# A two-block transformer on one core: the first pair's fourth weight sum by accumulating transfer, in all five feed-forward layers

## The reference, cut to what matters

```
gate, up = split(x @ w_gate_up)          # 1024 -> 2 * 2816
h = h + norm((silu(gate) * up) @ w_down) # 2816 -> 1024 (the first layer has no norm here)
```

## Time and profile before

| | |
|---|---|
| median of three executions | 1267.11 us |
| the profiled execution's own time | 1267.36 us |
| its span, first to last instruction | 1265.5 us |
| TensorE busy | 1250.5 us, 99% |
| VectorE busy | 1042.0 us, 82% |
| ScalarE busy | 804.2 us, 64% |
| granted TensorE clock, mean | 1.00 |
| moved by transfers | 277.32 MB, mean 219 GB/s |

### The profile page before, as it was taken

One profiled execution on the slowest core, in us unless ns is written; L12 is line 12 of the kernel. 1 busy time (PEld: TensorE's weight loads), 2 busy tenths in 40 slices (PEclk: granted clock), 3 DMA queues, 4 the chain that ended last, 5 costly groups with the idle time before them and its releaser, 6 DMA issues.

```text
span 1265.5 us, 15538 instructions
## 1 busy us (share of the span) xinstructions
PE 1250.5 (99%) x5897; PEld 1029.7 (81%) x5897; DVE 1042.0 (82%) x1035; ACT 804.2 (64%) x986; POOL 194.5 (15%) x224
## 2 busy tenths in 40 slices
PE   9999999999999999999999999999999999999998
PEld 7888878888888878888788888888888877788886
DVE  6766689999789996757799997999977568999984
ACT  6674576666576664645766664766656467766662
POOL 6142130110001100202201101111001003301100
PEclk9999999999999999999999999999999999999999
DMA  9537498997649955568979978389745535999931
GB/s 335 174 101 227 131 315 255 260 270 262 199 144 252 268 171 196 177 238 204 330 248 245 273 249 262 118 239 274 218 166 179 182 123 172 314 288 260 266 135 45
DMA packets 143002, 277.32 MB, mean 219 GB/s; under 512 B 8992, under 2 KB 39896, under 8 KB 142928
## 3 DMA queue, kind: packets, MB, share of 16 engines
q1 hardware_dynamic: 120192, 229.67, 51.5%
q0 software_dynamic: 22288, 45.54, 19.4%
q10 hardware_dynamic: 448, 1.12, 0.2%
HBM read 275.24 MB, written 1.05 MB: 218 GB/s over the span
## 4 chain that ended last, share of the span: by engine, by line
PE 83%; DVE 10%; issue 3%; ACT 3%; DMA 1%; POOL 0%; DVEq 0%; POOLq 0%; SPq 0%; ACTq 0%
PE B L2102 14%; PE B L2104 14%; PE B L2103 14%; PE B L2560 7%; PE B L2558 7%; PE B L2559 7%; DVE w_lo L1359 5%; PE T L2102 3%; PE T L2104 3%; PE T L2103 3%; PE T L2582 1%; DVE VD L1378 1%; ACT w_hi L768 1%; ACT w_hi L1082 1%; DMA VD<-in_ffn_w_gu 1%
## 5 line engine op out<-in xcount | busy, mean ns | idle before, releaser
L1359 DVE TENSOR_TENSOR w_lo<-w_raw,w_hi 128x2048 fp32r<-128x2048 f32 x129 | 296.5, 2300 | 87.2 <-ACT w_hi L768 86.9
L768 ACT ACTIVATE w_hi<-w_raw 128x2048 fp32r<-128x2048 f32 x129 | 247.2, 1919 | 103.2 <-PE B L2560 60.7
L2102 PE MATMUL B<-w_hi,xt_lo 128*128 128x512 f32 x652 | 260.2, 399 | 4.3 <-DVE w_lo L1359 2.2
L2104 PE MATMUL B<-w_hi,xt_hi 128*128 128x512 f32 x652 | 254.5, 390 | 0.0
L2103 PE MATMUL B<-w_lo,xt_hi 128*128 128x512 f32 x652 | 254.1, 390 | 0.0
L2558 PE MATMUL B<-w_hi,act_lo 128*128 128x512 f32 x440 | 172.5, 392 | 0.6 <-DVE w_lo L1359 0.6
L2560 PE MATMUL B<-w_hi,act_hi 128*128 128x512 f32 x440 | 171.4, 390 | 0.0
L2559 PE MATMUL B<-w_lo,act_hi 128*128 128x512 f32 x440 | 171.3, 389 | 0.0
L2102 PEld LDWEIGHTS B<-w_hi,xt_lo 128*128 128x128 f32 x652 | 122.5, 188 | 34.6 <-issue 4.4
L2104 PEld LDWEIGHTS B<-w_hi,xt_hi 128*128 128x128 f32 x652 | 122.4, 188 | 26.2
L2103 PEld LDWEIGHTS B<-w_lo,xt_hi 128*128 128x128 f32 x652 | 122.6, 188 | 23.2
(11 more groups left out here) (330 smaller groups left out, 2113.1 us busy)
## 6 DMA issues: line engine op xcount, KB each, us to landing
w_raw<-in_ffn_w_down SPq DMA_DIRECT2D x88, 512.0 KB, 5.7
Z<-in_ffn_w_gu SPq DMA_DIRECT2D x64, 512.0 KB, 7.8
w_raw<-in_ffn_w_gu SPq DMA_DIRECT2D x48, 512.0 KB, 5.1
nat<-in_ffn_w_gu SPq DMA_DIRECT2D x32, 512.0 KB, 7.7
QT<-in_ffn_w_gu SPq DMA_DIRECT2D x32, 512.0 KB, 7.0
Z<-in_ffn_w_gu POOLq DMA_DIRECT2D x32, 512.0 KB, 8.6
w_raw<-in_conv_w_in SPq DMA_DIRECT2D x24, 512.0 KB, 4.9
...
```

Of the source, the lines that this page charges most:

```text
L768: act.activation(whi[home(u)][:, :], raw[slot][:, :], ACT.Copy).then_inc(w_hi, 1)
L1359: dve.tensor_tensor(wlo[home(u)][:, :], src, whi[home(u)][:, :].bitcast(F32), ALU.subtract).then_inc(w_lo, 1)
L2102: pe.matmul(bank[:, :], lo[:, k, x], whi[s][:, c], start=first, stop=False, skip_group_check=more)
L2104: return pe.matmul(bank[:, :], hi[:, k, x], whi[s][:, c], start=False, stop=last, skip_group_check=more)
```

## The change

T4 of p = 0 joins those that are formed by an accumulating transfer, in all five layers (`FIRST_T4`). VectorE's sum for it is gone, GpSimd issues two more transfers of 512 KB in each layer, after the split of P6, and SyncE's load of the next B21 no longer waits for T4. Besides this, some orders are different: VectorE splits N1b ahead of `x_sums` (in all layers but the second), and the total of the activations is taken in two halves in layer 0 also; ScalarE does the first gate ahead of the high part of the activations' sums, loads the table of Silu earlier with a small instruction in layers 0 and 4, and in layer 4 squares h after N1b's split; ahead of layer 2 the split of N0b stands between the two halves of the squares and of the update; ahead of layer 4 the split of N0a stands ahead of `heads_lo(3)`, and TensorE's products of the output projection stand in another order.

The diff, cut to what the text speaks of:

```diff
--- before.py
+++ after.py
@@ -64,11 +64,17 @@
 
 SUMS = ((1, "T1"), (1, "T2"), (2, "T1"), (2, "T2"), (3, "T1"), (3, "T2"), (3, "T4"))
 ADDED_T4 = (1, 2)
+FIRST_T4 = (0, 1, 2, 3, 4)
+
+
+def added_t4(f):
+
+    return ((0,) if f in FIRST_T4 else ()) + ADDED_T4
 
 
 def sums_of(f):
 
-    return (((0, "T1"), (0, "T2")) if f % 2 else ()) + ((0, "T4"),) + SUMS
+    return (((0, "T1"), (0, "T2")) if f % 2 else ()) + (() if f in FIRST_T4 else ((0, "T4"),)) + SUMS
 
 
 def sums_ready(f, p, name):
@@ -78,7 +84,7 @@
 
 def t4_added(f, p):
 
-    return 32 * (len(ADDED_T4) * f + ADDED_T4.index(p) + 1)
+    return 32 * (sum(len(added_t4(g)) for g in range(f)) + added_t4(f).index(p) + 1)
 
 
 def down_block(name, p):
...
@@ -446,7 +453,7 @@
 
                     if p + 1 < SQUARES or next_gu is not None:
                         sp.wait_ge(w_lo, u0 + OP[reader, p] - 1)
-                        if name == "B21" and p == 0:
+                        if name == "B21" and p == 0 and f not in FIRST_T4:
                             sp.wait_ge(t_ok, sums_ready(f, 0, "T4"))
                         block_in(name, (p + 1) % SQUARES, w_gu if p + 1 < SQUARES else next_gu)
 
@@ -625,9 +632,11 @@
 
             def add_blocks(f, w_gu, p0=0):
 
+                if p0 and 0 in added_t4(f):
+                    add_block("T4", f, 0, w_gu)
                 for p in range(p0, SQUARES):
                     add_block("T3", f, p, w_gu)
-                    if p in ADDED_T4:
+                    if p in added_t4(f):
                         add_block("T4", f, p, w_gu)
 
             def post_gain(b, layer, i):
...
@@ -794,12 +803,14 @@
                 waits = [(in_x[t], 16)] * 2 if reader == "x" else [(h_up, h_ready(reader, t, half)) for half in range(2)]
                 tok_squares(stat, lambda t, half: h[:, t, half * HALF:half * HALF + HALF], t, waits)
 
-            def sum_squares(stat, reader, u_last, late_split=None, gain=0, pairs=PAIR, early=4):
-
-
-
-                tok_squares(stat, lambda t, half: pairs[half][t][:, :], 0,
-                            [sum_done(reader, u_last, 0, half) for half in range(2)])
+            def sum_squares(stat, reader, u_last, late_split=None, gain=0, pairs=PAIR, early=4, between=()):
+
+
+
+                waits = [sum_done(reader, u_last, 0, half) for half in range(2)]
+                tok_squares(stat, lambda t, half: pairs[half][t][:, :], 0, waits, (0,))
+                split_at(*between)
+                tok_squares(stat, lambda t, half: pairs[half][t][:, :], 0, waits, (1,))
                 if late_split is not None:
                     split_at(*late_split)
                     turned_hi(reader, lambda k: gain + k, 0, 0, early)
@@ -1057,9 +1068,8 @@
                     turned_hi(reader, lambda k: gain + k, 1)
                     if f != 1:
                         split_at(u0 + 2)
-                    if f == 4:
-                        h_squares(stat, reader, 0)
-                    h_squares(stat, reader, 1)
+                    if f != 4:
+                        h_squares(stat, reader, 1)
 
                 def weights(name, p=0):
                     split(u0 + OP[name, p])
@@ -1074,7 +1084,7 @@
                         act.wait_ge(t3_in, 32 * (n + 1))
                     elif src in ("T1", "T2") and p == 0 and f % 2 == 0:
                         act.wait_ge(*((t1_in, 32 * f + 64) if src == "T1" else (t2_in, 16 * f + 32)))
-                    elif src == "T4" and p in ADDED_T4:
+                    elif src == "T4" and p in added_t4(f):
                         act.wait_ge(t4_in, t4_added(f, p))
                     else:
                         act.wait_ge(t_ok, sums_ready(f, p, src))
@@ -1119,12 +1129,17 @@
                     act.activation(act_parts(d)[0][:, :], act_bank(d)[:, :], ACT.Copy).then_inc(act_hi, 1)
 
                 weights("N1b")
+                if f == 4:
+                    for t in range(TOKS):
+                        h_squares(stat, reader, t)
                 block("P1", 0)
+                if f in (0, 4):
+                    act.activation(table[:, f // 4:f // 4 + 1], gains[:, G_ONE:G_ONE + 1], ACT.Silu)
+                act.wait_ge(rstd, 2 * ST[stat] + 2)
+                gate_of(0, u0 + OP["N0b", 0], PAIR[0] if f else F0)
                 act.wait_ge(sx_ok, f + 1)
                 act.wait_ge(w_used, u0 + OP["N0b", 0] + 1)
                 act.activation(yhi[:, :, :], xsum, ACT.Copy).then_inc(sx_hi, 1)
-                act.wait_ge(rstd, 2 * ST[stat] + 2)
-                gate_of(0, u0 + OP["N0b", 0], PAIR[0] if f else F0)
                 block("P2", 0)
                 gate_of(1, u0 + OP["N1b", 0], GU)
                 act_out(0)
@@ -1226,8 +1241,8 @@
             copy_t1(2)
             conv_hi(2)
             conv_hi(3)
-            split_at(*range(U_COUT + 2, U_COUT + 6))
-            sum_squares("y1", "ffn2", U_COUT + 3, (), n2(0, 4), early=8)
+            split_at(*range(U_COUT + 2, U_COUT + 5))
+            sum_squares("y1", "ffn2", U_COUT + 3, (), n2(0, 4), early=8, between=(U_COUT + 5,))
             ffn(2, "h5", "ffn2", n2(0, 4), k0=8)
             sum_squares("y2", "ffn3", U_FFN[2] + FFN_UNITS - 1, (), n2(1, 0), early=8)
             ffn(3, "h6", "ffn3", n2(1, 0), 8, kv=True)
@@ -1402,6 +1417,15 @@
                 turned_lo(name, gain_cols, 1)
                 split_at(u0 + 2)
 
+            def x_total(name, t0=0, t1=TOKS):
+
+                dve.wait_ge(xt_lo, XT[name] + t1 * KD)
+                x = slice(t0 * P, t1 * P)
+                steps[0] += 1
+                dve.tensor_tensor(xsum[:, :, x], xhi[:, :, x].bitcast(F32), xlo[:, :, x].bitcast(F32), ALU.add)\
+                    .then_inc(dve_step, 1)
+                return steps[0]
+
             def evac(e, u_last, dst, pair, stat):
 
                 dve.wait_ge(w_used, u_last + 1)
...
@@ -1447,6 +1471,8 @@
 
                     dve.wait_ge(ssq, 4 * ST[stat] + 2 * t + half + 1)
                     ins = dve.tensor_tensor(tmp[:, half, :], pairs[half][t][:, :], gpost[:, c], ALU.mult)
+                    if half == 0:
+                        split_at(*between)
                 link(ins)
                 dve.wait_ge(rstd, 2 * ST[stat] + t + 1)
                 for half in range(2):
@@ -1712,6 +1738,7 @@
             turned_lo("ffn0", lambda k: G_FFN + k, 0, 0, 4)
             mem_out_lo(1)
             turned_lo("ffn0", lambda k: G_FFN + k, 0, 4)
+            x_total("ffn0", 0, 1)
             split_at(21)
             h_update("ffn0", U_MO + 1, 1, MOP)
             turned_lo("ffn0", lambda k: G_FFN + k, 1)
...
@@ -1764,7 +1780,7 @@
                         x_total(reader, 0, 1)
                         turned_lo(reader, lambda k: gain + k, 1, 4)
                         split_at(u0 + 2)
-                    total = x_total(reader, 1, 2)
+                total = x_total(reader, 1, 2)
 
                 def weights(name, p=0):
                     u = u0 + OP[name, p]
@@ -1814,8 +1830,12 @@
                     hi, lo = act_parts(d)
                     dve.tensor_tensor(lo[:, :], act_bank(d)[:, :], hi[:, :].bitcast(F32), ALU.subtract).then_inc(act_lo, 1)
 
-                x_sums(total)
-                weights("N1b")
+                if f == 1:
+                    x_sums(total)
+                    weights("N1b")
+                else:
+                    weights("N1b")
+                    x_sums(total)
                 block("P1", 0)
                 dve.wait_ge(rstd, 2 * ST[stat] + 2)
                 act_of(0, PAIR[0] if f else F0)
@@ -1827,7 +1847,8 @@
                 block("P5", 0)
                 block("P6", 0)
                 block("P3", 0)
-                weight_sum("T4", f, 0)
+                if f not in FIRST_T4:
+                    weight_sum("T4", f, 0)
                 block("P7", 0)
                 weights("D0")
                 block("P4", 0)
...
@@ -1942,8 +1963,8 @@
             conv_gate(3)
             conv_lo(2)
             conv_lo(3)
-            split_at(*range(U_COUT + 2, U_COUT + 6))
-            ffn(2, "h5", "ffn2", n2(0, 4), lambda t: post_update(1, "y1", "ffn2", t))
+            split_at(*range(U_COUT + 2, U_COUT + 5))
+            ffn(2, "h5", "ffn2", n2(0, 4), lambda t: post_update(1, "y1", "ffn2", t, between=() if t else (U_COUT + 5,)))
 
             ffn(3, "h6", "ffn3", n2(1, 0), lambda t: post_update(2, "y2", "ffn3", t), kv=True)
 
@@ -2077,8 +2098,9 @@
             split_at(U_O + 3)
             o_sum(3)
             o_norm(3)
+            split_at(U_O + 4)
             heads_lo(3)
-            split_at(U_O + 4, U_O + 5)
+            split_at(U_O + 5)
             ffn(4, "h8", "ffn4", n2(1, 4), lambda t: post_update(4, "y4", "ffn4", t, AO))
             for t in range(TOKS):
                 post_update(5, "y5", "out", t)
@@ -2875,22 +2897,21 @@
             for k in (4, 5):
                 out_heads(1, k, 0)
             heads_pair(3)
-            for k in (4, 5):
-                out_heads(0, k, 1)
+            for half in range(2):
```

(8 more changed lines are left out.)

20 lines of the change are left out of this document (6 added, 14 removed).

## The result

The changed kernel takes 1293.49 us (median of five executions, 1290.85 to 1296.19) against 1267.42 us, now of five executions too: a ratio of 1.0201, 95% interval 1.0188 to 1.0215. It is 26 us slower, where the forecast was 13.5 us slower with a range that ended at 1292.

The account below looks back on a forecast made before the run. The prediction took TensorE to bound the kernel: 1267.36 us + 16.5 lost at D1 - 3.0 gained by the orders = 1280.9 us, given as 1280.6 for the median, range 1270 to 1292.

Parts of the forecast that it names:

- D1 has no slack: At TensorE's D1: whatever delays VectorE between P4's low part and `act_out(1)` delays TensorE by as much.
- The chain of 10.6 us: From P4's high part to D1: VectorE's splits and sums, `act_lo` and the step to the matmul sum to 10.6 us.
- The orders gain: N1b's split ahead of the sums and the transposes ahead of layers 2 and 4: 3.0 us gained, 1 to 4.
- The removed sum: VectorE's addition for T4 ahead of P7's low part: costs TensorE 0.41 us a layer, 2.0 us in all.
- the lag: From P6's low part to P4's high part, waiting for T4's landing: 10.5 us, ends 10.4 and 11.5.
- the 16.5 us of D1: At D1 in five layers: start 21.1 us after P6's low part instead of 17.8, 3.3 us lost each.
- 9.6, which I took for the lag of a lightly loaded queue: Rival at T4's transfer, faster at p = 0 with less queued: lag 9.6 us, 2.4 us lost a layer, 1276.1 us; chance 0.10.
- The forecast's own range: Whole kernel: 1276 to 1287 us from lag 10.4 to 11.5 us and gains 1 to 4; chance 0.59.
- The clock: Rival at D1: TensorE's idle 3.5 us drops its clock to 1.2 GHz, 5.4 us a layer, 1308 us; chance 0.03.
- hardly late: At P4: its low part ends 14.8 us after P6's, at 210.8 in layer 0; TensorE comes to it at 210.6.
- The transfer lands in time: Rival at T4's landing before P4: D1 not delayed, gain 3.0 + 2.0, 1262.1 us; chance 0.08.
- The rival on B12: At T1 of p = 1: T4's traffic delays B12's load, about 1 to 2 us more a layer, 1286 to 1291 us; chance 0.16.

Follow-up runs that it names:

- e11: Changed kernel with T4 of the first pair by transfer in layer 2 only: 1270.82 us, ratio 1.0021.
- e1: Changed kernel with the new orders alone, VectorE summing T4 of the first pair again in all layers: 1265.21 us, ratio 0.9973.
- e7: Changed kernel without T4 in the first pair, neither transfer nor sum nor wait (output differs): 1262.65 us, ratio 0.9961.
- e4: Changed kernel with VectorE's C22 and C12 ahead of P4's low part and the sum T1 behind act's low part: 1292.65 us, ratio 1.0188.
- e2: Kernel before with only T4 of the first pair by accumulating transfer, its own orders kept: 1296.92 us, ratio 1.0221.
- e5: Changed kernel with TensorE repeating matmuls in the gaps before P4 and D1 of the first pair (output differs): 1291.05 us, ratio 1.0177.
- e12: Changed kernel with SyncE issuing the next pair's B12 ahead of B22 and B21, behind P7's low part: 1279.06 us, ratio 1.0100.
- e3: Changed kernel with the next pair's loads of B22, B21 and B12 held until T4 has landed: 1300.71 us, ratio 1.0247.
- e8: e7 plus T4's two transfers into other memory, for which nothing waits before the third pair (output differs): 1290.37 us, ratio 1.0178.
- e9: e7 with P4's high part on ScalarE waiting for half of D0, nothing transferred: 1292.10 us, ratio 1.0185.
- e10: e8 with SyncE issuing the next pair's B12 ahead of B22 and B21: 1265.84 us, ratio 0.9983.

## Why the prediction was wrong

**What held.** TensorE is the bound, D1 has no slack, and what VectorE loses ahead of `act_lo` TensorE loses: e11 has it for one layer, and the changed profile in all five. The chain of 10.6 us from P4's high part to D1 measured 10.6 in four layers and 11.25 in layer 2. The orders gain 3.1 us against 3.0 (e1): the waits at N1b and ahead of layer 2's transposes are gone, and the one ahead of layer 4's is still 0.7 us. The removed sum is worth what P7 waits, 2.0 us: e7 lies 5.2 us below its kernel before and e1 3.1, so 2.1.

**The step that failed** is the lag: "I take 10.5 us", because "the load beside it is like that at p = 0". It was 12.2, 13.2, 10.5, 12.3 and 10.3 us. Summed over the layers that is 6.0 us more, and with 0.65 us in layer 2's chain the 16.5 us of D1 become the measured 23.1. The 0.65 us in layer 2 are the wait for B12.

What is loaded beside T4 is at first the same block as at p = 1, but it comes sooner. B22 is issued when P3's low part is written. At p = 0 VectorE goes from P6's low part straight to P3's; at p = 1 it stands still for 0.40 us between them. SyncE's issue of B22 in layer 0, at p = 0 of the changed kernel, at p = 1 of the kernel before, and at p = 1 of e4:

```profile
197.13 1.14 SPq L432 DMA_DIRECT2D nat<-in_w_gate_up  x2
...
227.01 0.99 SPq L425 DMA_DIRECT2D nat<-in_w_gate_up  x2
...
228.34 1.17 SPq L432 DMA_DIRECT2D nat<-in_w_gate_up  x2
```

These are 2.27, 2.72 and 2.23 us after P6's low part. Over all layers, with the loads in their old order unless said (us after P6's low part; in the first two rows from the changed kernel, e2, e4, e5 and e11):

| T4 of | B22 issued | lag |
|---|---|---|
| p = 0, 17 cases | 2.26 to 2.32 | 11.6 to 13.2 |
| p = 0, 4 cases, two of them layers 2 and 4 of the changed kernel | 2.36 to 2.49 | 10.3 to 10.6 |
| p = 1, e4, 5 layers | 2.23 | 11.6 to 12.5 |
| p = 1, kernel before, 5 layers | 2.70 to 2.72 | 10.1 to 11.4 |
| p = 0, e12, 5 layers, B12 first | 6.9 to 7.4 | 8.9 to 9.1 |
| p = 0, e3, 5 layers | held until T4 has landed | 8.9 to 9.2 |

A third block, B21, is loaded beside T4 at p = 0 and not at p = 1, where it is issued only after T4 has landed (237.83 in e4). It isn't what makes the lag long: layers 2 and 4 of the changed kernel have it and a short lag, p = 1 of e4 has a long one without it. The regularity is not clean: at p = 1 and 2 of the other runs, with B22 after 2.6 us or more, most lags are 10.2 to 11.6 us, but single ones reach 12.2, and in e8, whose transfers go elsewhere, one landed after 12.1 us with B22 after 2.45.

What is lost is seen in one microsecond, from 6.0 us after P6's low part, when the first of T4's two transfers is ending. q0 is the queue of GpSimd's transfers, q1 that of SyncE's loads (packets, MB, share of the engines); first p = 0 of the changed kernel, then p = 1 of the kernel before, both in layer 0:

```profile
q1 hardware_dynamic: 149, 0.29, 82.8%
q0 software_dynamic: 6, 0.01, 11.0%
...
q0 software_dynamic: 60, 0.12, 65.4%
q1 hardware_dynamic: 52, 0.11, 33.3%
```

In that microsecond T4 got next to nothing at p = 0. No run moves B22's issue alone, so its part in the lag is read from the traces and not shown by experiment, and why 0.4 us should make this difference stays open. With the loads held, or the first of them issued 3.6 us later, the lag is 8.9 to 9.2 us in every layer: 9.6, which I took for the lag of a lightly loaded queue, was not even the lower end.

The forecast's own range is not what its ends give, either: a lag of 10.4 us with 4 us gained is 1279 us and not 1276, and 11.5 us with 1 us gained is 1288.

**The clock** was a rival at 0.03 with 5.4 us a layer. The fall came, but in the changed kernel it costs 1.6 us where it lies in D1 and nothing where it lies in P4. In the changed profile the stretches from D1 to the next down product are 2.1 us longer in all than before. 23.1 + 2.1 - 2.7 (the span of e1 against the earlier trace rows) is 22.5 of the 23.5 us between the spans. 1.0 us is left; between D1 of layer 1 and P6 of layer 2 TensorE has four small waits for low parts of weights and for h, 1.8 us in all, where e1 has two, 0.6 us. The median lies 2.6 us above this execution; in the profiles of e2 and e5 layer 2 landed after 12.4 and 13.0 us instead of 10.5 (B22 issued after 2.27 and 2.29 us instead of 2.36), so the landings differ between executions, but that this is the 2.6 us is argued and not shown.

**P4** was not "hardly late" (14.8 us against 14.6). TensorE's P4 waits for C22 as well, which stands behind P4's low part on VectorE: 12.2 + 2.0 + 2.2 + 0.6 + 0.1 = 17.1 us after P6's low part. I had not read that wait in the code. It costs nothing itself, since D1 is later, but it opens the gap in which the clock falls.

**The rivals.** "The transfer lands in time" was priced wrongly: its 1262.1 us is the time without transfer (e7, 1262.65), and with the transfer, if nobody waits for it, the time is 1290.37 (e8). The rival on B12 was right about the mechanism and wrong to be added on top. I worked out 17.3 us for B12's landing; in e8 T1, which waits for it, starts 17.7 to 18.8 us after P6's low part. In four layers of the changed kernel T1's turn comes later than that, so the two delays overlap instead of adding; only layer 2 pays 0.57 us on top. Taking away the wait alone brings 3.1 us (e8) and taking away the traffic alone 1.4 us (e9), of the 26; with the wait gone and B12 first all but 3 us come back (e10 against e7).
